# Hybrid attention block, one core: the merge-gate projection by Strassen's seven half-size products, interleaved with the head projections

## The reference, cut to what matters

```python
h = rmsnorm(x, g_norm[l])                       # x: (1, 256, 2048)
z = jnp.einsum('bsd,dn->bsn', h, w_in)          # w_in: 2048 x (8*1024 + 8 + 2*2048)
qa, ka, va, ga, qb, kb, vb, gb, fl, ma, mb = jnp.split(z, idx, axis=-1)
...                                             # 8 differential heads (a), 8 forgetting heads (b)
ya = jnp.einsum('bsw,wd->bsd', oa * silu(ga), w_proj_a)
yb = jnp.einsum('bsw,wd->bsd', ob * silu(gb), w_proj_b)
m = jax.nn.sigmoid(ma) * ya + jax.nn.sigmoid(mb) * yb
return jnp.einsum('bsd,de->bse', m, w_out)      # then x + that, then a last RMSNorm
```

## Time and profile before

| what | value |
|---|---|
| median of 3 runs | 762.22 us (761.75 to 762.23) |
| profiled execution: time, span of its trace | 762.72 us, 760.9 us |
| PE busy | 751.2 us, 99% of the span |
| DVE, ACT, POOL busy | 422.1, 365.8, 76.3 us |
| TensorE clock granted | 0.998 of full |
| traffic | 143.8 MB, mean 189 GB/s |

### The profile page before, as it was taken

One profiled execution on the slowest core, in us unless ns is written; L12 is line 12 of the kernel. 1 busy time (PEld: TensorE's weight loads), 2 busy tenths in 40 slices (PEclk: granted clock), 3 DMA queues, 4 the chain that ended last, 5 costly groups with the idle time before them and its releaser, 6 DMA issues.

```text
span 760.9 us, 9586 instructions
## 1 busy us (share of the span) xinstructions
PE 751.2 (99%) x3632; PEld 628.7 (83%) x3632; DVE 422.1 (55%) x616; ACT 365.8 (48%) x556; POOL 76.3 (10%) x153
## 2 busy tenths in 40 slices
PE   8999999999999999999999999999999999999996
PEld 6898888888888888888888888888888888888886
DVE  6754555555555566566665564444445666565552
ACT  6563554445544555445545554443444443444541
POOL 0001111101121221122202000000000000001110
PEclk9999999999999999999999999999999999999999
DMA  8747554554555545554545555555555555855642
GB/s 315 267 159 257 175 185 165 169 191 166 182 174 171 177 166 171 179 178 164 184 166 167 178 173 183 189 192 194 194 194 193 192 180 193 347 193 191 189 145 111
DMA packets 39885, 143.80 MB, mean 189 GB/s; under 512 B 4568, under 2 KB 4576, under 8 KB 39328
## 3 DMA queue, kind: packets, MB, share of 16 engines
q1 hardware_dynamic: 38576, 139.81, 54.8%
q10 hardware_dynamic: 1008, 1.84, 0.7%
q0 software_dynamic: 256, 1.54, 0.5%
HBM read 141.06 MB, written 2.11 MB: 188 GB/s over the span
## 4 chain that ended last, share of the span: by engine, by line
PE 96%; issue 1%; DMA 1%; DVE 0%; ACT 0%; DVEq 0%; POOLq 0%; POOL 0%; ACTq 0%
PE Z L219 29%; PE Z L221 29%; PE Z L220 29%; PE Z L340 3%; PE A L285 1%; PE A L253 1%; PE B L267 1%; PE Dk L276 1%; PE B L264 1%; DMA g_col<-in_g_cols 1%; PE C L294 0%; PE B L302 0%; PE A L302 0%; DVE w_lo L621 0%; ACT w_hi L422 0%
## 5 line engine op out<-in xcount | busy, mean ns | idle before, releaser
L621 DVE TENSOR_TENSOR w_lo<-w_raw,w_hi 128x1024 fp32r<-128x1024 f32 (+1 forms) x252 | 309.6, 1231 | 302.6 <-ACT w_hi L422 300.8
L422 ACT ACTIVATE w_hi<-w_raw 128x1024 fp32r<-128x1024 f32 (+1 forms) x247 | 261.6, 1060 | 348.2 <-PE Z L221 343.1
L219 PE MATMUL Z<-w_hi,hT_hi 128*128 128x512 f32 (+2 forms) x880 | 337.8, 384 | 0.4 <-DVE w_lo L621 0.4
L221 PE MATMUL Z<-w_hi,hT_lo 128*128 128x512 f32 (+2 forms) x880 | 335.3, 381 | 0.0
L220 PE MATMUL Z<-w_lo,hT_hi 128*128 128x512 f32 (+2 forms) x880 | 335.1, 381 | 0.0
L219 PEld LDWEIGHTS Z<-w_hi,hT_hi 128*128 128x128 f32 x880 | 165.4, 188 | 32.0 <-issue 0.6
L221 PEld LDWEIGHTS Z<-w_hi,hT_lo 128*128 128x128 f32 x880 | 165.4, 188 | 31.9
L220 PEld LDWEIGHTS Z<-w_lo,hT_hi 128*128 128x128 f32 x880 | 165.5, 188 | 30.5
L219 PE MATMUL Z<-w_hi,oT_hi 128*128 128x512 f32 x128 | 50.1, 391 | 0.0
L221 PE MATMUL Z<-w_hi,oT_lo 128*128 128x512 f32 x128 | 49.9, 389 | 0.0
L220 PE MATMUL Z<-w_lo,oT_hi 128*128 128x512 f32 x128 | 49.8, 389 | 0.0
(11 more groups left out here) (161 smaller groups left out, 485.2 us busy)
## 6 DMA issues: line engine op xcount, KB each, us to landing
w_raw<-in_w_main SPq DMA_DIRECT2D x251, 512.0 KB, 3.3
w_raw<-in_w_fl SPq DMA_DIRECT2D x4, 528.0 KB, 4.5
x_sb<-in_x SPq DMA_DIRECT2D x1, 2048.0 KB, 9.2
x_sb<-in_xT ACTq DMA_DIRECT2D x4, 256.0 KB, 7.4
x_sb<-in_xT SPq DMA_DIRECT2D x4, 256.0 KB, 5.6
rows<-c_rows_dram POOLq DMA_DIRECT2D x1, 1024.0 KB, 6.2
rows<-in_g_final SPq DMA_DIRECT2D x1, 1024.0 KB, 11.2
out_y<-gates SPq DMA_DIRECT2D x2, 384.0 KB, 2.5
```

Of the source, the lines that this page charges most:

```text
L219: pe.matmul(acc, a_hi, b_hi, start=first, stop=False)
L221: return pe.matmul(acc, a_lo, b_hi, start=False, stop=last)
L422: act.activation(w_hi[:, t % RING, 0:n], w_raw[:, t % RING, 0:n], ACT.Copy).then_inc(hi_ready, 1)
L621: dve.tensor_tensor(w_lo[:, t % RING, 0:n], w_raw[:, t % RING, 0:n], w_hi[:, t % RING, 0:n].bitcast(fp32), ALU.subtract).then_inc(lo_ready, 1)
```

## The change

The 8 merge chunks are taken as 4 pairs (`g` = 0 to 3): the chunk of `ma` and the chunk of `mb` for the same 512 columns. For such a pair the product is a 2 x 2 block product: token blocks 0 and 1, input rows in a near and a far half (8 slices each), and the two column chunks. Strassen's scheme (in Winograd's form) computes it with 7 half-size products ("forms" P1 to P7) where the plain way has 8. The parts of the change are:

- **PE.** A form has 4 tiles (`q` = 0 to 3) of 6 matmuls each, all into one bank, Z2 or Z3 in turn (`sum_tile`). The stationary operand is `hT` or one of four precomputed sums of activation blocks, `sum_hi` and `sum_lo`.
- **Loads and splits.** Each of the 4 x 7 x 4 = 112 form tiles is loaded at its full 512 KB and split by ACT and DVE as before. There were 64 merge tiles.
- **Weight sums.** Forms P5, P6, P7 and P4 need sums of weight blocks, each made from the one before and a new load. DVE adds the tiles of P5 and P7 (32 adds of [128 x 1024]), POOL those of P6 and P4 (32 adds). The running sum is `chain`, which lies in `x_sb` (x is loaded again at the end).
- **Eviction.** P1 and P5 are copied out by ACT (`keep`). The other forms are added into `gates` by DVE (`fold`, 7 adds of [128 x 512] a pair), and then ACT applies tanh in place.
- **Order.** A block of 16 jobs holds the 8 tiles of one head chunk (3 to 15, then the first two projection chunks of branch b) and 8 form tiles, at the steps `HEAD_STEPS` and `SUM_STEPS`. The heads have banks Z0 and Z1. ACT and DVE split for job+4, DVE adds for job+5, POOL adds for job+7.
- **Start.** POOL multiplies x by g in 8 steps of [128 x 512], ahead of `rstd`, and then builds the four activation sums (4 ops of [128 x 1024]). ACT and DVE split these into high and low.
- **Others.** The second chunk has 8 smaller loads where it had 4. The attention outputs of heads 0 to 12 are stored in f32 and split later, in 4 wide ops on ACT and DVE, where DVE had `gated_lo` for each head. The branch-b projections run first, then those of branch a.

In the diff, cut to its core, `sum_tile` is PE's, the loop over `job` is DVE's, and what follows it is POOL's.

```diff
+def sum_parts(s):
+    return s // (FORMS * QUARTERS), s // QUARTERS % FORMS, s % QUARTERS
...
+            def sum_tile(s):
+                g, f, q = sum_parts(s)
+                job = SUM_JOB[s]
+                pe.wait_ge(hi_ready, job + 1)
+                pe.wait_ge(lo_ready, job + 1)
+                if q == 0:
+                    fill = FORMS * g + f
...
+                        form_taken(fill - 2)
...
+                acc = Z[2 + (FORMS * g + f) % 2]
+                for kk in range(2):
...
+                    mm = split_product(acc[:], stat_hi, stat_lo, hi[:, kk], lo[:, kk],
+                                       k == 0, k == TILES - 1)
+                mm.then_inc(w_used, 1)
...
+            for job in range(PLAIN_JOB, DIFF_JOB):
+                if job in HEAD_OF and HEAD_OF[job][1] == TILES - 1:
+                    evacuate(HEAD_OF[job][0])
...
+                    fold(*sum_parts(SUM_OF[job])[0:2])
+                if job + 5 in SUM_OF and sum_parts(SUM_OF[job + 5])[1] in (P5, P7):
+                    add(SUM_OF[job + 5])
+                split(job + RING)
...
+            for j in range(TILES):
+                pool.wait_ge(xl_ready, 2 * j + 2)
+                pool.wait_ge(x_squared, j + 1)
+                sl = slice(2 * j, 2 * j + 2)
+                pool.tensor_tensor(xT_sb[:, sl, :], xT_sb[:, sl, :], g_col[:, sl].unsqueeze(2).to_broadcast([P, 2, SEQ]),
+                                   ALU.mult).then_inc(h_scaled, 1)
             pool.wait_ge(ms_ready, 1)
             pool.tensor_tensor(rstd[:], ms[:], neg_half[:], ALU.pow).then_inc(rstd_ready, 1)
...
+            def add(s):
+                g, f, q = sum_parts(s)
+                job = SUM_JOB[s]
+                if f == P6:
+                    pool.wait_ge(lo_ready, SUM_JOB[s - QUARTERS] + 1)
+                else:
+                    pool.wait_ge(added, add_no(s - QUARTERS))
+                wait_raw(pool, job)
+                pool.tensor_tensor(chain[:, q, :], raw_slot(job), chain[:, q, :], ALU.subtract).then_inc(pool_added, 1)
```

More of the change, by code:

```diff
@@ L23 @@
 RING = 4
+RAW = 4
 TILES = 8
@@ L343, in _ @@
                 mm.then_inc(w_used, 1)
-            for j in range(4):
-                tile(8 + j, 1, hT_hi, hT_lo, 4 * j, 4, FL_COLS, j == 0, j == 3)
-                if j == 1:
+            for j in range(TILES):
+                tile(FL_JOB + j, 1, hT_hi, hT_lo, 2 * j, 2, FL_COLS, j == 0, j == TILES - 1)
+                if j == 3:
                     pe.wait_ge(x_summed, TILES - 1)
@@ L355, in _ @@
             for j in range(4):
[L356 to L359, removed]
-                    z_tile(c, j)
[L361 to L365, removed]
-                        pe.matmul(B[:, HEADS:2 * HEADS], tri, log_f[:, 1, :], start=False, stop=True).then_inc(c_done, 1)
-                    if c == 2 and j == 1:
-                        pe.wait_ge(c_nat_ready, 1)
-                        for m in range(M_TILES):
-                            mm = pe.matmul(C[0:HEADS, m * P:(m + 1) * P], c_nat[:, m, :], ident, start=True, stop=True)
-                        mm.then_inc(cT_done, 1)
-                    if c == 2 and j == 5:
-                        pe.wait_ge(c_neg_ready, 1)
-                    attention(c, j)
@@ L376, in _ @@
[L376 to L385 removed]
+                tile(VG_JOB + j, 0, hT_hi, hT_lo, 4 * j, 4, 2 * HD, j == 0, j == 3)
@@ new lines, in _ @@
+            banks_free(3)
+            for j in range(TILES):
+                z_tile(2, j)
+                if j == 0:
+                    pe.wait_ge(log_f_ready, 1)
+                    pe.matmul(B[:, 0:HEADS], tri, log_f[:, 0, :], start=True, stop=True)
+                    pe.matmul(B[:, HEADS:2 * HEADS], ones, log_f[:, 0, :], start=True, stop=False)
+                    pe.matmul(B[:, HEADS:2 * HEADS], tri, log_f[:, 1, :], start=False, stop=True).then_inc(c_done, 1)
+                if j == 1:
+                    pe.wait_ge(c_nat_ready, 1)
+                    for m in range(M_TILES):
+                        mm = pe.matmul(C[0:HEADS, m * P:(m + 1) * P], c_nat[:, m, :], ident, start=True, stop=True)
+                    mm.then_inc(cT_done, 1)
+                if j == 5:
+                    pe.wait_ge(c_neg_ready, 1)
+                attention(head_job(2, j))
@@ new lines, in _, with fox_tile @@
+            for job in range(MIXED_JOB, FOX_JOB):
+                if job in HEAD_OF:
+                    c, j = HEAD_OF[job]
+                    if j == 0:
+                        banks_free(4 if c == 3 else fill_of(c) + 1)
+                    z_tile(c, j)
+                else:
+                    sum_tile(SUM_OF[job])
+                attention(job)
+            def fox_tile(n, j):
+                if j == 0:
+                    banks_free((18, 19, 19, 20)[n])
+                    if n == 2:
+                        form_taken(FORMS * GROUPS - 2)
+                        form_taken(FORMS * GROUPS - 1)
+                if n == 0:
+                    pe.wait_ge(o_split, j // 2 + 1)
+                tile(fox_job(n, j), 1 if n == 2 else 0, oT_hi, oT_lo, 2 * j, 2, CHUNK, j == 0, j == 3)
@@ new lines, in _ @@
+            for job in range(FOX_JOB, DIFF_JOB):
+                if job in FOX_OF:
+                    fox_tile(*FOX_OF[job])
+                else:
+                    sum_tile(SUM_OF[job])
+                attention(job)
+            for n in range(4):
+                banks_free(21 + n)
+                for j in range(4):
+                    if n == 0:
+                        pe.wait_ge(o_split, 3 if j < 2 else 4)
+                        if j >= 2:
+                            pe.wait_ge(oT_lo_ready, 1 if j == 2 else 3)
+                    tile(diff_job(n, j), 1 - n % 2, oT_hi, oT_lo, HEADS + 2 * j, 2, CHUNK, j == 0, j == 3)
+                    attention(diff_job(n, j))
@@ L658, in _ @@
                     x_sum(j - 3)
-            for j in range(4):
-                split(8 + j)
+            for j in range(TILES):
+                split(FL_JOB + j)
                 if j < 3:
```

605 lines of the change are left out of this document (402 added, 203 removed).

## The result

The changed kernel takes 774.70 us (median; 771.40 to 778.58), the kernel before 762.17 us beside it: a ratio of 1.0168, interval 1.0145 to 1.0190. It is 12.5 us slower; 751.4 us had been forecast. Its runs spread wider than those of before, and those with the lower granted clock are the longer ones (0.994 at 771.40, 0.987 at 778.58, which is the profiled one).

A forecast was written before the change was run, and what follows sets the result against it. PE was taken to bound the kernel, busy for 99% of the span. 762.7 - 21.8 + 5 (start) + 5 (sums) + 1 (seam) = 751.9 us against the profiled execution, 751.4 as a median; range 740.5 to 760.5 us.

The forecast's parts named there:

- 96 matmuls less: Merge chunks on PE: four pairs save 96 matmuls of 0.227 us each, 21.8 us in all.
- Loads: Form tile loads: land after 3.3 us, costed at nothing; rival that they take 6.4 us: 762 us, chance 0.03.
- "I take 5 us" for the sums: POOL's weight sums for P6 and P4: PE waits because POOL holds DVE up, 5 us taken.
- Both ends: POOL's weight sums: DVE loses 0.2 us a meeting, 0 us for PE, or 2.6 us every sum, some 17 us.
- cushion of 3.0 us: Mixed blocks: DVE may be 3.0 us late with a tile's low part before PE stands still.
- The start: POOL's eight multiplies beside DVE's gapless first-chunk run: 5 us taken; the four activation sums after them: 0.
- the bound of 6.8: First chunk: if POOL's eight multiplies (10.4 us) hold DVE up in full, less 3.6 us of room, PE loses 6.8 us.
- The seam: Third projection chunk, right behind the last form tile: PE waits for its fold, 0.7 us and two hand-overs, 1 us.
- The clock: PE's granted clock, 1.00 before: the forecast would be wrong if it fell below 1.00; no time was added for it.
- 740.9: PE work alone, against the profiled execution: 762.7 - 21.8 = 740.9 us.
- Slower: Rival: every sum holds DVE its whole length; start 6.8, sums 17, seam 1 make 765.7 us; chance 0.11.
- The 0.2 us of the one meeting: Earlier trace: a DVE split begun while POOL multiplied took 1.42 us where 1.23 is usual; lower price of the sums.

The follow-up runs named there:

- the best version: Kernel before the change, with the change plus all weight and activation sums on DVE, last fold ahead, POOL's scalings behind `rstd`: 749.05 us, ratio 0.9823.

## Why the prediction was wrong

**What held.** 96 matmuls less, 0.227 us each, one bank or two, as forecast: the best version lies 8.7 us above 762.2 - 21.8 = 740.4, and PE's idles in it after the first 12 us, none over 1.22, sum to 6.3. Loads: they landed after 4.2 us where it was 3.3, and cost nothing that the runs show. DVE's own adds: 759.65 against 758.60 us, 1 us, no more than the runs vary. POOL was busy for 191 us, as said; DVE for 576 and not 540, since held ops count as busy (28 us of it: 547.5 us without POOL's sums).

**The step that failed first: "I take 5 us" for the sums.** They cost 15.05. The range for it, 0 to 17, held, but by luck: another mechanism than the one I priced filled it. Both ends were worked out from DVE being held, against a cushion of 3.0 us; held it was, and the cushion covered nearly all of it. What I did not price is the sum itself on the way of its tile: load lands, POOL adds for 2.69 us (where DVE takes 1.22), ACT rounds, DVE subtracts, PE. The cushion was counted from the moment at which PE frees a slot, as if the sum were there by then. I had even written that the two sums behind the rotary ops hold ACT and its whole queue up, and used it as a mark for the choice and not as a term. ACT waited 43.1 us for POOL, which points there. By itself that row proves nothing: with all sums on DVE, ACT waited 32.3 us for them, and the kernel was 13.4 us faster. The mark that I had named told it as well: I had written that PE's waits for `w_lo` would gather in the phases of P6 and P4, and in the blocks they are mostly for `w_hi`, 7 times and 6.8 us, against twice and 1.8 us for `w_lo`.

**The start: 5 us taken, 9.7 measured, over the bound of 6.8.** That bound covered the scalings alone. The activation sums were costed at nothing, "where DVE is half idle". That it was, 4.43 us of the 10 from 40 to 50; but in the window from 45 to 50 us of the changed kernel DVE, held, is busy for 4.99 of 5.00. Moving these sums to DVE gave 4.8 us. The scalings' place gave some 2 by difference, not clear of the spread, so the shares of the two stay open. The mark was missed too: the last first-chunk matmuls were to begin 4 to 7 us after 29.17, if I was right on the start, and began 2.5 us after it, with PE waiting for `w_lo` as I had said.

**The seam: 1 us taken, 5.4 measured.** I added a fold and two hand-overs, and did not read what stands ahead of the fold in DVE's queue. An order of the queue showed it.

**The clock.** It was named as a thing that would make the forecast wrong, and not priced. In the changed kernel it fell behind the idles of 2.91, 2.06, 2.17 (at 388 us) and 5.02 us, 1.5 to 3 us of work each. In the profiled run half of the time at the lower clock, counted from where PE goes on, makes 1.7 us behind each of the first three and 2.8 behind the last: some 8 of the 37.7 us that it lies above 740.9 (an estimate). That run had the lowest clock; what the granted clock of the whole run takes off its span is 10.1 us there (0.987) and 7.0 us in the runs near the median (0.991), which is most of why these are shorter (an estimate too). Each term above holds its own part of this share.

The three terms as measured make 740.4 + 15.05 + 9.7 + 5.4 = 770.5; the other 4 us are not assigned to a place, and the terms are not known better than that. The rival *Slower* came nearest with its sum (765.7) and with its 17 us for the sums; its start (6.8) was too low. Its mechanism, DVE held for the whole of each sum, is nearer to what happened in the experiment with ops beside DVE's own sums than to what the changed kernel does.

**The rule of the Trainium skill** ("SBUF — State Buffer", section "SBUF: two separate sides": one of the two holds the port pair and the other waits) is borne out on DVE's side: the add of the squares (`z_sb<-o_T` in the rows of the start) took 1.58 us where it had taken 0.68, and `half_rstd` 2.36 us, each beside one of POOL's ops; `half_rstd` reads one SBUF tensor only, which is not the case that I had quoted. The 0.2 us of the one meeting in the earlier trace rows was no guide. But 24 ops held DVE for 23.2 us and cost PE 2.3: the step from held engine to lost time needs the cushion.

## What to carry to other kernels

A helper engine's op is not free when its engine is idle: ask who waits for its result, how much longer it takes there (2.69 against 1.22 us), and what stands behind the waiter in an in-order queue. To tell a shared port from a late result, run the op with nobody waiting for it; but do so in the same surroundings, since the same 24 ops cost 2.3 us in one kernel and 17.8 in another whose DVE made the awaited sums. Where PE bounds a kernel, add to a PE idle of 2.6 us or more some 1.5 to 3 us for the clock behind it (behind one of 2.0 to 2.3 us it came in two cases of seven here), and read the whole queue ahead of any op that PE waits for.

## What the hardware showed that I had not expected

The granted clock of TensorE fell from 1.00 to 0.50 after idles of 2.81 and 3.61 us in a kernel that otherwise never left 1.00, about 1 us after PE had gone on; in the idles of 5.21 and 7.61 us it fell before PE had gone on. It stayed at 1.00 after 1.15 us. Near 2 us it goes either way. The profiled executions of the changed kernel, of the one without the start's work and of the one with the fold ahead hold seven idles of 2.0 to 2.3 us: it fell behind 2.06 and 2.17, and not behind 2.17 (564.03), 2.10, 2.27, 2.10 and 2.00. What decides stays open; it may be a part of the spread between runs, which no run shows apart.

An op of DVE that touches two elements of each partition can take as long as the POOL op beside it (2.36 us), so small ops between the large ones are held too.
